# Two experts side by side in 64x64 pieces of the TensorE array, in a decoder layer with product-key experts

## What is computed

```python
s = jnp.einsum('...qhgd,...khd->...hgqk', q, k) * (HEAD_DIM ** -0.5)    # windowed attention, 8 heads of 64

q = (xt @ w_pq).reshape(128, 8, 2, 128)                # expert retrieval, for a block of tokens
s = jnp.einsum('thcd,hckd->thck', q, sub_keys)
s1, i1 = top_k(s[:, :, 0], 16);  s2, i2 = top_k(s[:, :, 1], 16)
top, sel = top_k(s1[..., None] + s2[..., None, :], 16) # best 16 of 256 pairs
idx = take_along_axis(i1 * 128 + i2, sel)              # 16 of 16384 experts, per token and head
gate = softmax(top)
h = einsum('td,thkd->thk', xt, u_tab[idx])             # dot with the row of u
a = gelu(h) * gate
out = einsum('thk,thkd->td', a, v_tab[idx])            # weighted sum of the rows of v
```

## Time and profile before

| | us |
|---|---|
| median of 3 runs | 1921.02 (1917.58 to 1921.38) |
| the profiled execution: its own time | 1911.93 |
| the profiled execution: span, first to last instruction | 1909.9 |
| PE busy | 1628.8 (85%) |
| DVE busy | 1157.2 (61%) |
| ACT busy | 826.8 (43%) |
| POOL busy | 644.7 (34%) |
| mean granted TensorE clock | 0.967 of full |

### The profile page before, as it was taken

The page is one execution under the profiler, slowest core; times in us unless marked ns, Lnnn a source line. Parts: engine busy times, 40 slices in busy tenths (PEclk is TensorE's granted clock), DMA queues, the critical chain, the costliest instruction groups (busy, mean ns, idle before and its releaser), DMA issues.

```text
span 1909.9 us, 16797 instructions
## 1 busy us (share of the span) xinstructions
PE 1628.8 (85%) x4760; PEld 800.3 (42%) x4760; DVE 1157.2 (61%) x2716; ACT 826.8 (43%) x2312; POOL 644.7 (34%) x583
## 2 busy tenths in 40 slices
PE   7997988887898888888888888888888888888876
PEld 5555556644444333433333433333433334333322
DVE  2223453446656676666776667776667767667754
ACT  2203333255555554544444444445444445544443
POOL 0000000132434434444444444444444444444442
PEclk9997999999989999999999999999999999999999
DMA  9301006496989999999999999999999999999997
GB/s 309 133 1 56 1 1 216 163 337 233 353 330 347 388 412 393 421 412 414 420 416 411 419 418 416 416 412 406 421 414 422 421 417 414 402 418 417 417 421 301
DMA packets 106933, 646.32 MB, mean 338 GB/s; under 512 B 12128, under 2 KB 25224, under 8 KB 32072
## 3 DMA queue, kind: packets, MB, share of 16 engines
q0 software_dynamic: 83056, 604.28, 78.0%
q1 hardware_dynamic: 23784, 40.97, 6.2%
HBM read 642.00 MB, written 4.19 MB: 338 GB/s over the span
## 4 chain that ended last, share of the span: by engine, by line
PE 53%; DMA 21%; DVE 12%; ACT 7%; issue 6%; POOL 0%; SPq 0%; ACTq 0%; DVEq 0%; POOLq 0%
PE ps L1539 30%; DMA R<-in_peer_uv,R 19%; PE ps L1167 12%; PE ps L1498 6%; DVE R L1123 4%; ACT R L698 2%; ACT L689 1%; ACT R L693 1%; DVE R L1048 1%; DMA R<-in_peer_sub_keys 1%; DVE R L1076 1%; DVE R L1045 1%; DVE R L1071 1%; DVE R L1079 1%; PE ps L1519 1%
## 5 line engine op out<-in xcount | busy, mean ns | idle before, releaser
L1539 PE MATMUL ps<-R 128*128 128x512 f32 x2304 | 1122.1, 623 | 231.8 <-ACT R L698 226.1
L472 POOL DMA_INDIRECT R<-in_peer_uv,R x576 | 642.6, 1116 | 969.4 <-PE ps L1539 847.5
L1123 DVE CUSTOM_DVE_ANT_0 R<-R 128x1024 f32<-128x1024 f32 x576 | 699.0, 1225 | 395.4 <-DMA R<-in_peer_uv,R 385.7
L1539 PEld LDWEIGHTS ps<-R 128*128 128x128 f32 x2304 | 418.4, 195 | 845.5 <-ACT R L698 508.8
L689 ACT ACTIVATE R<-R 128x1 f32<-128x1 f32 x576 | 115.4, 200 | 547.4 <-DVE R L1123 539.2
L698 ACT ACTIVATE R<-ident,R 128x128 f32<-128x128 f32 x512 | 205.6, 402 | 47.7 <-ACT R L693 0.4
L693 ACT ACTIVATE R<-R 128x1 f32<-128x1 f32 x576 | 169.8, 295 | 20.9
L1498 PE MATMUL ps<-A,xT 128*128 128x256 f32 x640 | 145.3, 379 | 0.8 <-ACT xT L627 0.8
L1498 PEld LDWEIGHTS ps<-A,xT 128*128 128x128 f32 x640 | 121.4, 190 | 35.1 <-issue 20.8
L1167 PE MATMUL ps<-A,xT 128*128 128x512 f32 (+1 forms) x320 | 121.2, 539 | 0.0
L461 POOL MEMSET R<- 128x512 f32 x1 | 0.5, 527 | 272.4 <-PE ps L1297 272.4
(11 more groups left out here) (213 smaller groups left out, 1040.5 us busy)
## 6 DMA issues: line engine op xcount, KB each, us to landing
R<-in_peer_uv,R POOLq DMA_INDIRECT x576, 9.7
A<-in_w_peer_q SPq DMA_DIRECT2D x2, 4096.0 KB, 15.7
A<-in_w_in SPq DMA_DIRECT2D x3, 2048.0 KB, 18.2
R<-in_w_out SPq DMA_DIRECT2D x1, 4096.0 KB, 14.2
x_res<-in_x_prompt SPq DMA_DIRECT2D x4, 512.0 KB, 13.7
R<-in_cache_mem_k SPq DMA_DIRECT2D x8, 256.0 KB, 4.3
R<-in_cache_mem_v SPq DMA_DIRECT2D x8, 256.0 KB, 5.7
out_y_p<-R SPq DMA_DIRECT2D x4, 512.0 KB, 8.3
```

The lines of the kernel that those rows point to most:

```text
L472: pool.indirect_dma_start(slots[g % SLOTS], None, I["peer_uv"][:, :], bass.IndirectOffsetOnAxis(ap=idx[:, b % 4, k:k + 1], axis=0)).then_i ...
L1123: dve.tensor_tensor_reduce(u_rows[g % SLOTS], u_rows[g % SLOTS], xn[:, t * D:(t + 1) * D], 1.0, 0.0, ALU.mult, ALU.add, hdot[:, b % 2, k:k ...
L1539: ins = pe.matmul(bank(2 * (t % 2) + c), diag[:, g % DIAGS, :], v_rows[g % SLOTS][:, c * 512:(c + 1) * 512], start=first, stop=last)
```

## The change

Four edits.

1. **The expert product in quarters.** Only the diagonal of `diag` is not zero, so the two off-diagonal quarters of the array multiply zeros. PE now treats two experts, g and g + 1, at once, at odd k: expert g goes to the quarters rows 0-63 to columns 0-63 and rows 64-127 to columns 64-127, expert g + 1 to the other two. Each is a 64x64 matmul of 512 columns, eight matmuls for a pair of experts, in the order written below. The lower rows add into banks 0 and 1, the upper rows into banks 2 and 3, for every tile. A pair waits for `diag` of the later expert; the slots of both are given back near its end.
2. **`diag` is 128x64**, two 64x64 diagonals on top of one another, made from `fold` for all tiles, with six buffers instead of four.
3. **`add_acc`** is four DVE operations of 64x1024 instead of one of 128x1024, some of them chained by a wait, at k = 1 instead of 3. Since all tiles share the four banks, the first pair of a tile waits on PE for it (`acc_added`).
4. **The attention scores** take the heads in the order 0, 4, 1, 5, 2, 6, 3, 7.

```diff
-DIAGS = 4
+DIAGS = 6
+HALF = 64
@@ scalar: diagonal
-                base = fold if b < 4 else ident[:, :]
-                act.activation(diag[:, g % DIAGS, :], base, ACT.Copy, scale=coef[:, b % 2, col])\
+                act.activation(diag[:, g % DIAGS, :], fold[:, 0:HALF], ACT.Copy, scale=coef[:, b % 2, col])\
                    .then_inc(diag_ready, 1)
@@ vector: add_acc
                 dve.wait_ge(v_used, tile_end(t))
-                q = 2 * (t % 2)
-                dve.tensor_tensor(xr(t), xr(t), ps[:, q * 512:(q + 2) * 512], ALU.add).then_inc(acc_added, 1)
+                lo, hi = slice(0, HALF), slice(HALF, P)
+                sums = ((lo, lo, 0), (lo, lo, 1024), (lo, hi, 0), (lo, hi, 1024)) if t == 0 else \
+                    ((lo, lo, 0), (hi, hi, 1024), (lo, hi, 0), (hi, lo, 1024))
+                for n, (to, part, a) in enumerate(sums):
+                    ins = dve.tensor_tensor(xr(t)[to], xr(t)[to], ps[part, a:a + 1024], ALU.add)
+                    if n in ((0, 1, 2) if t == 0 else (1,)):
+                        chain(ins)
+                ins.then_inc(acc_added, 1)
@@ vector: the loop over k
-                    if k == 3 and b > 0 and starts_tile(b):
+                    if k == 1 and b > 0 and starts_tile(b):
                         add_acc(t - 1)
@@ tensor: attention scores
-                for h in range(HEADS):
+                for h in (0, 4, 1, 5, 2, 6, 3, 7):
@@ tensor: experts
-            def expert(b, k):
+            def expert_pair(b, k):
                 g, t = b * TOPK + k, tile_of(b)
-                first, last = starts_tile(b) and k == 0, g + 1 == tile_end(t)
-                if first and t >= 2:
-                    pe.wait_ge(acc_added, t - 1)
-                pe.wait_ge(diag_ready, g + 1)
+                first, last = starts_tile(b) and k == 0, g + 2 == tile_end(t)
+                lo, hi = slice(0, HALF), slice(HALF, P)
+                if first and t >= 1:
+                    pe.wait_ge(acc_added, t)
+                pe.wait_ge(diag_ready, g + 2)
                 for c in range(2):
-                    ins = pe.matmul(bank(2 * (t % 2) + c), diag[:, g % DIAGS, :],
-                                    v_rows[g % SLOTS][:, c * 512:(c + 1) * 512], start=first, stop=last)
-                ins.then_inc(v_used, 1)
+                    for n, (e, rows, to) in enumerate(((g, lo, lo), (g, hi, hi), (g + 1, lo, hi), (g + 1, hi, lo))):
+                        acc = bank(c if rows is lo else 2 + c)
+                        ins = pe.matmul(acc[to], diag[rows, e % DIAGS, :],
+                                        v_rows[e % SLOTS][rows, c * 512:(c + 1) * 512], start=first, stop=last)
+                        if c == 1 and n % 2 == 1:
+                            ins.then_inc(v_used, 1)
@@ tensor: the loop over k
                     beside(b, k, cross, ffn)
-                    expert(b, k)
+                    if k % 2 == 1:
+                        expert_pair(b, k - 1)
```

More of the change, by code:

```diff
@@ L186, in hybrid_step @@
         fold = R[:, 20480:20608]
-        diag = v3(R[:, 20608:21120], DIAGS)
+        diag = v3(R[:, 20608:20992], DIAGS)
         ss = v3(R[:, 21632:21888], 2)
```

## The result

The changed kernel takes **2090.35 us** (median of 4 runs, 2086.64 to 2102.82) against 1921.2 us of the kernel before on the same chip: a ratio of 1.089, 95% interval 1.084 to 1.094. It is slower by 169 us, where I had forecast 26. The profiled execution has a span of 2084.8 us, 174.9 more than before.

What follows compares the result with a forecast made beforehand. Gathers, not PE, were taken to set the even stage's pace, through how early slots return. Terms -2 + 0 + 17 + 7 + 4 = +26 us on 1921 gave 1947 us, range 1900 to 1995.

Steps and rivals of the forecast that it cites:

- the term of +17 us: Blocks from 5 on: gathers late through held slots and low clock, net 0.55 us in each of 31 blocks.
- The pair on PE: Expert product: four 64x64 quarters run at once, so two experts take 2.15 us where they took 3.70.
- two rounds of two quarters: Rival on the expert product: pieces overlap only in part, a pair takes 3.65 us, total 2030 us; chance 0.07.
- The held slot at the upper clock: Behind expert 10: slot reissued 6.03 us before its gather is due, 5.7 to 7.0 needed; 0.3 us late.
- The clock: Pair (10, 11) after longer PE idle: lower clock in half of the blocks, gather then 1.9 us late.
- the rival of the low clock: Pairs and queries run at the lower clock: some 6 us in a block, 190 in all, 2110 us; chance 0.08.
- The first five blocks: Stretch from 375 to 660 us: nothing gained or lost, 0 us, bounds -10 and +8.
- The handshake: First five blocks: the second expert's diagonal releases the next step, with or without the first, so pairing gains nothing.
- The change of tile: Four sums instead of one make the first pair of a tile wait: 1.75 us each, +7 us, bounds 0 and +12.
- The end: Last sums of the kernel, covered by nothing: 4 x 1.22 against 1.22 us, +4 us.
- The attention scores: Low and high halves overlap: 16 records in 1.9 instead of 2.94 us in three tiles; -2 us, bounds -4 and 0.
- One reading of the page: Profile of the kernel before: PE busy 85% of the span, half of it on one line.

Runs made afterwards that it cites:

- e10: The changed kernel's 64x64 quarters and four sums with one expert at a time, but both slots of a pair given back by the second expert: 2006.80 us, ratio 1.044.
- e1: The changed kernel without the pairing: same quarters, four sums and attention order, but each expert has its own wait and slot release: 1936.38 us, ratio 1.009.
- e3: The changed kernel with unused filler products on PE behind most pairs from block 5 on: 2036.32 us, ratio 1.059.
- e7: e1 with only the first of the four sums at a tile change, so part of the output is missing: 1920.84 us, ratio 1.001.
- e4: The kernel before with five slots in place of six, nothing else: 2013.58 us, ratio 1.047.
- e8: The kernel before with only the attention scores reordered to heads 0, 4, 1, 5, 2, 6, 3, 7: 1915.58 against 1918.22 us, ratio 0.9987.
- e9: e8 with DVE's work behind experts 10 and 12 cut in halves behind 9 to 12: 1911.29 against the kernel before's 1918.22 us, ratio 0.9958.

## Why the prediction failed

The direction was right, and the mechanism, a slot that is held for its partner, is right for 70 of the 169 us. The size was not: 2090 us lies far beyond 1995. The step that failed is the term of +17 us (bounds -17 and +66) for the held slot and the low clock: in the blocks 5 to 35 the hold costs 67 us (e10 against e1) and what the pair does on PE another 63 (changed kernel against e10), 130 in all. By the medians of the runs the 169 us split into 15 (the sums, e1), 70 (the held slot, e10 against e1) and 84 (what the pair does on PE, after against e10). Of the last, the filler of e3 brings 54 back: all but 9 of the 63 us in the blocks 5 to 35, and none of the 17.5 in the blocks 0 to 4, where it has no filler.

**The pair on PE: right.** 1.95 us, where I wrote 2.15 (2.0 to 2.3 as what to see), and PE's busy share in the even stage fell from 85% to 60%. The Trainium skill (TensorE: Matmul & The Clock Gate, Part 3, The mechanism) has it that a weight load overlaps with running products only if its row group differs. By that, read as two rounds of two quarters (the prediction's estimate), the two experts, which share both row halves, would have taken 3.65 us; the row has 1.95 at the upper clock. The measurement decides, for fp32 pieces of this size.

**The held slot at the upper clock: right place, wrong size.** I gave the place behind expert 10 a slot life of 8.87 us, a needed lead of 5.7 to 7.0, and chose 0.3 us of lateness. In e10 the life is 9.1 us where the clock did not fall (a lead of 5.8) and up to 10.8 where it did, and the gather takes 5.7 to 6.8 us in 18 of the 29 blocks 5 to 33: 1.2 us late in block 17. Then I closed the account, but the next gather comes another 0.8 us late, and I subtracted 0.56 us for what the kernel before loses. That made -0.26 us where e10 lost 2.2. The needed lead of the earlier trace rows was about right; taking a value near the lower end of the lateness, at a place where only 6.03 us were left, was the error. Its upper bound of 0.9 with the 0.8 that follows would have made 1.7 x 31 = 53 us.

**The clock: the part that was furthest off.** I counted half of the blocks with one slow pair each, 1.9 us. The life of 10.84 us in block 24 is my number (8.87 + 1.8, lead 4.1 where I wrote 4.3), but 23 of 29 blocks have over 10.2, and 58% of all pairs are slow, not only that one. A slow pair elsewhere has a lead of 7.65 - 1.75 = 5.9 us, which I had not worked out; the table by expert has 8, 10, 12 and 14 late by 0.3 to 0.5 us each against e1. I dismissed the rival of the low clock (2110 us, a chance of 0.08) because falls of the clock in the trace before ended when PE was busy. But PE in the changed kernel is idle again after each pair: of the 65 pairs after a gap of 2 to 3 us, 60 were slow, of the 99 after 1 to 2 us 21. The length of one gap doesn't decide it: the products of 11 and 12 in e1, behind 2.2 us of idle PE, were slow in 9 of 26 blocks. The rival's own account isn't right either: it put 190 us on the clock alone, and e3 gives back 54.

**The first five blocks: wrong.** 0 us (-10 to +8) was the forecast, +24 came. e1 takes 5.8 of them, the held slot adds 1.0 (e10), and the pair itself 17.5. The 5.8 are not the sums at the first change of tile, since e7, which leaves three of four out, has 269.1 us here. Some 3 us of them may be the spread of single traces: the kernels of e4, e8 and e9, which are the kernel before with small edits, have 264.2 to 264.4 where it has 261.7. The handshake was read rightly, nothing was gained, but the pair that ends such a handshake now begins only with the second diagonal, and the clock there is 0.81 instead of 0.95, so that 13 of the 40 pairs take 3.7 us. That the clock is the cause in these blocks is argued, not shown: no run had filler there.

**The change of tile: too small.** 1.75 us each, +7 for four. e1 against before has +5.6, +4.1 and +4.0 us in the pairs of blocks 12 and 13, 20 and 21, 28 and 29 (45.5 + 41.2 against 40.1 + 41.0, and so on), some 14 in all, and e7 takes all but 0.9 of it back. The likely reason is that four sums delay DVE's next dots, and with them more than one slot. PE's wait for them in the changed kernel (us in all, times, longest):

```profile
PE ps L1548 <- DVE x_res L1104: 15.4, 3, 6.5
```

**The end: right.** +3.6 us where I wrote +4; the last sums:

```profile
2070.38 1.95 PE L1548 MATMUL ps<-R 64*64 64x512 f32 x16 [1.52 <-ACT R L698]
...
2072.42 4.94 DVE L1104 TENSOR_TENSOR x_res<-x_res,ps 64x1024 f32<-64x1024 f32 x4 [3.10 <-PE ps L1548]
```

**The attention scores: not contradicted, and not shown.** -2 us (-4 to 0); the first dot starts 0.8 us earlier, and e8 gives -2.6 us with an interval that holds zero.

One reading of the page was off, without any weight in the sum: line 1539 has 1122.1 of PE's 1628.8 busy us, 69% and not half.

What stays open: why the second gather behind a hole lands 3.25 to 3.30 us after the first although it had been issued 8.0 us ahead (e10, 1202.36 to 1210.35); and how the 17.5 us of the blocks 0 to 4 split between the clock and the later start. A seventh slot, which would test the cushion from the other side, wasn't tried.

## What to carry to other kernels

Where transfers set the pace, an engine's speed counts only through the moment at which it gives a buffer back: write down the life of a buffer at the most disturbed place of the loop, not at the even one, and give any lead that is near the measured need its full lateness, the neighbours' included. Work that is batched into fewer, shorter bursts leaves PE idle in between, and here 117 of the 125 bursts behind more than 2 us of idle PE were slow; where a trace before shows such falls, price most of the bursts at 1.2 GHz. A batch that waits for its last member pays for both. Before such a change, one run in which only the release is delayed (e10) gives a good part of the price, here 70 of the pair's 154 us.

## What the runs showed of the hardware

- 16 fp32 records of 64x64 weights and 512 columns, four quarters of the array in turn, took 1.95 us at the granted clock of 1.00 and 3.69 us at 0.50, though two experts shared each row half. Two single experts in a queue, each in two quarters, overlap in part: 16 records in 3.08 us, alone 1.93 each; in full width two took 3.70. (e10:)

```profile
1202.31 3.08 PE L1548 MATMUL ps<-R 64*64 64x512 f32 x16 [0.17 <-ACT R L698]
...
1205.65 1.93 PE L1548 MATMUL ps<-R 64*64 64x512 f32 x8 [0.26 <-ACT R L698]
```

- The mean granted clock of the even stage went from 0.98 to 0.78 when PE's busy share fell from 85% to 60% in bursts; with filler (79%) it was 0.96.
- A pair behind 2 to 3 us of idle PE was slow (over 2.5 us, with the granted clock at 0.50 for part or all of it) in 60 of 65 cases in the changed kernel, and the products behind the gap of 2.2 us ahead of expert 11 in e1 in 9 of 26 blocks.
- A gather took 5.7 to 6.8 us in 18 of 29 blocks from issue to landing at the disturbed place of e10, against 5.70 with an empty queue; 7.8 us kept the even rhythm at the end of e4.
